# Scan of an RWKV-7 block: the last level of a blockwise inverse writes the turned inverse, without a turn on PE

## What is computed

```python
def wkv7_scan(S0, r, decay, kk, b, k, v, reverse, emit):
    def step(S, inp):
        r_t, w_t, kk_t, b_t, k_t, v_t = inp
        sa = jnp.einsum('bhvk,bhk->bhv', S, -kk_t)
        S = S * w_t[:, :, None, :] + sa[..., None] * b_t[:, :, None, :] + v_t[..., None] * k_t[:, :, None, :]
        y = jnp.einsum('bhvk,bhk->bhv', S, r_t) if emit else None
        return S, y
```

## Time and profile before

| | us |
|---|---|
| median of 3 runs | 4740.95 |
| lowest and highest | 4729.24, 4745.95 |
| profiled execution | 4736.67 |
| its span | 4734.9 |
| the scan in it, first to last PE record | 3108.7 to 3730.6 |

### The profile page before, as it was taken

How to read it: one execution, slowest core, us unless ns; L and a number is a source line. 1 busy time by engine, 2 the same in 40 slices (tenths; PEclk the granted TensorE clock), 3 DMA queues, 4 the chain that set the end, 5 groups by cost and what they waited for, 6 DMA issues and landing times. The chain is left out here.

```text
span 4734.9 us, 81944 instructions
## 1 busy us (share of the span) xinstructions
PE 4130.6 (87%) x34438; PEld 3392.6 (72%) x34438; DVE 2731.4 (58%) x4351; ACT 1748.5 (37%) x2865; POOL 329.5 (7%) x415
## 2 busy tenths in 40 slices
PE   6999986997898998699478897978999587999997
PEld 5878864886785667488366676768888466888886
DVE  2347736884774554789345013657777644466556
ACT  2136623774463442377346111223222112222222
POOL 0000000220000000021000000023233001000000
PEclk9999996998999999799689898969898789999998
DMA  2100037994000002899300201000000031111110
GB/s 100 45 9 2 2 114 292 376 397 147 19 2 1 1 13 98 314 397 382 124 20 19 89 30 59 25 8 3 3 3 3 26 142 54 45 54 36 54 45 40
DMA packets 139161, 425.62 MB, mean 90 GB/s; under 512 B 14660, under 2 KB 50380, under 8 KB 114220
## 3 DMA queue, kind: packets, MB, share of 16 engines
q1 hardware_dynamic: 129580, 386.83, 21.2%
q0 software_dynamic: 9216, 33.56, 2.8%
HBM read 370.03 MB, written 50.33 MB: 89 GB/s over the span
## 5 line engine op out<-in xcount | busy, mean ns | idle before, releaser
L557 PE MATMUL psum<-weight_parts,h_parts 128*128 128x512 f32 (+2 forms) x2880 | 601.0, 371 | 46.0 <-DVE weight_parts L703 29.6
L557 PEld LDWEIGHTS psum<-weight_parts,h_parts 128*128 128x128 f32 x2880 | 508.2, 192 | 132.9 <-DVE weight_parts L703 30.7
L1520 DVE TENSOR_TENSOR weight_parts<-weights_raw,weight_parts 128x2048 fp32r<-128x2048 f32 x192 | 431.8, 2288 | 57.5 <-ACT weight_parts L1490 55.4
L911 ACT ACTIVATE scores<-scores,softmax_stats 128x1024 f32<-128x1024 f32 (+2 forms) x288 | 307.9, 1069 | 329.7 <-DVE softmax_stats L956 329.6
L1490 ACT ACTIVATE weight_parts<-weights_raw 128x2048 fp32r<-128x2048 f32 x192 | 360.6, 1919 | 76.8 <-DMA weights_raw<-in_moe_w_up 46.1
L1428 PE MATMUL psum<-weight_parts,picked_parts 128*128 128x512 f32 x1536 | 365.0, 398 | 16.1 <-DVE weight_parts L1520 10.8
L1901 PE MATMUL psum<-h_parts,up_parts 128*128 128x512 f32 x1536 | 355.5, 393 | 11.0 <-DVE up_parts L1976 11.0
L1917 PE MATMUL psum<-down_parts,hidden_parts 128*128 128x512 f32 x1536 | 353.5, 391 | 6.7 <-DVE down_parts L1981 6.7
L1428 PEld LDWEIGHTS psum<-weight_parts,picked_parts 128*128 128x128 f32 x1536 | 291.5, 191 | 80.1 <-issue 11.5
L703 DVE TENSOR_TENSOR weight_parts<-weights_raw,weight_parts 128x2048 fp32r<-128x2048 f32 (+2 forms) x48 | 100.7, 2098 | 426.5 <-ACT weight_parts L612 426.5
L1901 PEld LDWEIGHTS psum<-h_parts,up_parts 128*128 128x128 f32 x1536 | 291.7, 190 | 72.5 <-DVE up_parts L1976 11.8
(11 more groups left out here) (437 smaller groups left out, 7243.1 us busy)
## 6 DMA issues: line engine op xcount, KB each, us to landing
weights_raw<-in_moe_w_gate SPq DMA_DIRECT2D x64, 1024.0 KB, 14.0
weights_raw<-in_moe_w_up SPq DMA_DIRECT2D x64, 1024.0 KB, 14.1
weights_raw<-in_moe_w_down SPq DMA_DIRECT2D x64, 1024.0 KB, 13.0
w_ada<-in_w_ada SPq DMA_DIRECT2D x12, 2048.0 KB, 11.2
up_raw<-in_w_mlp_up SPq DMA_DIRECT2D x16, 1024.0 KB, 7.2
down_raw<-in_w_mlp_down SPq DMA_DIRECT2D x16, 1024.0 KB, 4.9
weights_raw<-in_even_w_in SPq DMA_DIRECT2D x10, 1024.0 KB, 5.1
weights_raw<-in_w_in SPq DMA_DIRECT2D x10, 1024.0 KB, 5.2
```

Of the source, the lines that this page charges most:

```text
L557: last = pe.matmul(ps[:, t, 0:width(n)], cols[:, i, KP * h + k, t * P:(t + 1) * P], part[:, n % 2, j, k, 0:width(n)], start=(h == 0 and m ...
L911: act.activation(s_b[:, i % 2, a, 0:w], s_b[:, i % 2, a, 0:w], ACT.Exp, bias=st[:, i % 4, 0, a:a + 1], scale=-1.0, accum_out=st[:, i % 4, ...
L1520: dve.tensor_tensor(part[:, n % PART_SLOTS, 1], raw[:, n % RAW_SLOTS], part[:, n % PART_SLOTS, 0].bitcast(F32), ALU.subtract).then_inc(low, 1)
```

## The change

The last level no longer adds its block into `b.M`. What it wants is the inverse turned, and the new block turned is the product of the same two factors with their roles exchanged: the masked X as weights, and columns of `b.MT` as what is multiplied. The masked X of the last level is written into one half of a buffer `XW` of full width (64 columns), whose other half is cleared once by POOL, so that rows of the result that don't belong to the block come out zero. DVE adds the product into the second half of the columns of `b.MT` (`second_half`). The turn on PE, its copy on ACT and the round that both stood in go; `PHASES` goes from 26 to 25, and `LAG` stays 6. The counts of `m_ready` and `mt_ready` trade places (5 and 6 for each tile). POOL and DVE drop one idle round each.

```diff
-PHASES = 26
+PHASES = 25
...
+    WIDE = 115.5
...
+        b.XW = c.at("below_diagonal_wide", WIDE + n, [P, 4, 64])
...
+    first_half = lambda d: slice(32 * d, 32 * d + 32)
+    second_half = lambda d: slice(32 - 32 * d, 64 - 32 * d)
...
                     for level in range(5):
                         n = 5 * i + level
-                        pe.wait_ge(s["m_ready"], n + i + 1)
+                        pe.wait_ge(s["m_ready"], n + 1)
...
+                        if n == 4:
+                            pe.wait_ge(s["x_wide_cleared"], 1)
...
-                        pe.wait_ge(s["mt_ready"], n + 1)
+                        pe.wait_ge(s["mt_ready"], n + i + 1)
                         for h4 in range(4):
                             for cc, C in CH:
-                                last = pe.matmul(ps[C, B, h4 * 32:(h4 + 1) * 32], b.MT[C, h4], b.X[C, h4],
-                                                 start=True, stop=True)
+                                out = ps[C, B, h4 * 32:(h4 + 1) * 32]
+                                if level < 4:
+                                    last = pe.matmul(out, b.MT[C, h4], b.X[C, h4], start=True, stop=True)
+                                else:
+                                    last = pe.matmul(out, b.XW[C, h4], b.MT[C, h4, second_half(d)],
+                                                     start=True, stop=True)
                         last.then_inc(s["m_done"], 1)
                         yield
-                    pe.wait_ge(s["m_ready"], 6 * i + 6)
-                    for h4 in range(4):
-                        for cc, C in CH:
-                            last = pe.matmul(ps[C, A, h4 * 64:(h4 + 1) * 64], b.M[C, h4], c.ident[C, C],
-                                             start=True, stop=True)
-                    last.then_inc(s["mt_turned"], 1)
-                    yield
-                    pe.wait_ge(s["mt_copied"], i + 1)
+                    pe.wait_ge(s["mt_ready"], 6 * i + 6)
...
-                    act.wait_ge(s["mt_turned"], i + 1)
-                    act.activation(flat(b.MT), ps[:, A, 0:256], ACT.Copy).then_inc(s["mt_copied"], 1)
-                    yield
...
+                pool.memset(b.XW[:, :, second_half(d)], 0.0).then_inc(s["x_wide_cleared"], 1)
...
-                    for _ in range(14):
+                    for _ in range(13):
                         yield
...
-                        dve.tensor_tensor(b.X[:], ps[:, A, 0:128].rearrange("p (h n) -> p h n", h=4),
+                        below = b.X[:] if level < 4 else b.XW[:, :, first_half(d)]
+                        dve.tensor_tensor(below, ps[:, A, 0:128].rearrange("p (h n) -> p h n", h=4),
                                           wide(mask.levels[:, level]), ALU.mult).then_inc(s["x_masked"], 1)
...
+                        if level == 4:
+                            dve.wait_ge(s["mt_ready"], 6 * i + 5)
+                            target = b.MT[:, :, second_half(d)]
+                            dve.tensor_tensor(target, target, ps[:, B, 0:128].rearrange("p (h n) -> p h n", h=4),
+                                              ALU.add).then_inc(s["mt_ready"], 1)
```

More of the change, by code:

```diff
@@ L2350, in first_blocks @@
         return v[:, :, d, :] if len(a.shape) == 2 else v[:, :, :, d, :]
+    first_half = lambda d: slice(32 * d, 32 * d + 32)
+    second_half = lambda d: slice(32 - 32 * d, 64 - 32 * d)
     names = ("lora_done", "tanh_done", "log_ready", "running_ready", "exps_ready", "key_scaled", "key_ready", "scaled",
              "ends_scaled", "pairs_done", "pairs_masked", "bk_turned", "bk_copied", "lkv_done", "lkv_copied",
-             "mt_ready", "m_ready", "x_done", "x_masked", "m_done", "mt_turned", "mt_copied", "a_state_done", "z_ready",
+             "mt_ready", "m_ready", "x_done", "x_masked", "x_wide_cleared", "m_done", "a_state_done", "z_ready",
              "u_done", "u_ready", "decayed", "s_done", "state_ready", "y_started", "y_done", "tile_done", "state_cleared")
@@ L2633, in stream @@
                     dve.tensor_tensor(b.MT[:], b.MT[:], wide(eye[:]), ALU.add).then_inc(s["mt_ready"], 1)
-                    dve.wait_ge(s["mt_ready"], 5 * i + 1)
+                    dve.wait_ge(s["mt_ready"], 6 * i + 1)
                     dve.transpose(flat(b.M), flat(b.MT)).then_inc(s["m_ready"], 1)
@@ L2643, in stream @@
                         dve.wait_ge(s["m_done"], n + 1)
[L2644 to L2650, removed]
+                        if level == 4:
[3 more added lines that the diff above has]
+                                              ALU.add).then_inc(s["mt_ready"], 1)
+                        else:
+                            dve.wait_ge(s["m_ready"], n + 1)
+                            target = first_blocks(b.M[:], level, d)
+                            dve.tensor_tensor(target, target, ps[:, B, 0:128]
+                                              .rearrange("p (h g n) -> p h g n", h=4, n=2 << level), ALU.add)\
+                               .then_inc(s["m_ready"], 1)
+                            dve.wait_ge(s["m_ready"], n + 2)
                             dve.transpose(flat(b.MT), flat(b.M)).then_inc(s["mt_ready"], 1)
                         yield
-                    yield
                     for q, cc in enumerate((0, 1) if d == 0 else (1, 0)):
```

## The result

The changed kernel takes 0.987 of the time before (95% interval 0.9859 to 0.9885): medians 4671.5 and 4735.1 us, 61 us by the ratio. The forecast was 4721, its range 4702 to 4752. The profiled execution of the changed kernel took 4685.9 us, with a span of 4684.1; it is the longest of the four shown (the others took 4668.7 to 4673.1), so its rows hold a little more low clock than most executions: the clock over the span is 0.926 in it and 0.930 to 0.932 in the others.

The account below looks back on a forecast made before the run. In the scan neither PE (92% busy) nor DVE (72%) was taken to bound alone; a round lasts about as long as the slower needs. From 4736.7 us, -13.5 for nine tiles, -1 start and -1 tail gave 4721, range 4702 to 4752.

Parts of the forecast that it names:

- DVE's busy time per tile: Sign in the changed kernel's profile, steady part of the scan: DVE's busy time per tile stays at 43 us.
- The level-4 product, its mask and its add: Last level on PE and DVE: same shapes and element counts as before, so no change in time.
- ACT's copy and wait: ACT's 0.38 us copy of the turned inverse and its wait: removal gives nothing in the steady part, something in the tail.
- the weave's term: Scan, 26 rounds becoming 25: -1.3 us a tile, -1.5 with low clock, nine tiles, -13.5.
- table of loads: Sums of PE and DVE work in us for each round of a tile, for 26 and for 25 rounds.
- the one of the two that the text foresaw: Rounds 23 and 24: y's end, 1.75 us of PE, covers the masked pairs; PE's wait for them nearly goes.
- My two sums: Per tile: larger of PE's and DVE's load each round, +0.4 us; over overlapping neighbouring pairs of rounds, halved, -1.3.
- The terms for start and tail: First tile at half clock, double the turn's 0.47 us: -1 us; tail, turn, copy and wait fall away: -1 us.
- rival C: Scan: if rounds 7 to 9 reach 5.3 us, a third low-clock stretch per tile; +15, 4746 to 4765 us, chance 0.18.
- C's measure: Length of stretches with 3.9 us of PE work; for rounds 7 to 9 it decides between 4.6 and 5.3 us.
- each turn would then pay its slot: PE alone sets the pace, each turn gives 0.47 us at full clock: 4702 to 4711 us, chance 0.17.

Follow-up runs that it names:

- filled kernel before: Kernel before, turn and 26 rounds kept, with 16 matmul records that nobody reads added in round 3 of each tile and stream: 0.9943, 27 us faster.
- the last runs: Tiles at full clock: changed kernel with turn's records 52.5 us; same, distances 7, 6, 6, 6, 56.2; filled kernel before 57.0; before with DVE's bt merged, filled, 60.3.

## Why the prediction was wrong, point by point

**What held.** DVE's busy time per tile stayed (43.0 and 42.9 us). The level-4 product, its mask and its add cost what their forerunners did, ACT's copy and wait were free in the steady part (and the run without the copy), and the other stages didn't change.

**The failed step is the weave's term: forecast at -1.3 us a tile (-1.5 with the low clock), measured at -4.5.** At full clock a tile takes 57.0 us with 26 rounds (filled kernel before) and 52.5 with 25; with the low clock of each as it was, 59.6 and 54.0. The term stood in the sum with nine tiles, -13.5; the steady part alone, seven tiles, gave 39.2 us. Two of its inputs can be held against windows.

- By its table of loads rounds 1 to 3 get longer by the 1.1 us that DVE has more to do, and rounds 7 to 9 by 0.7. DVE was busy for 5.22 us in rounds 1 to 3, against 5.43 in the filled kernel before and 5.66 in the kernel before, and for 4.07 us in rounds 7 to 9, against 4.16: the added DVE work didn't fall into these stretches of PE's time.
- By the same table rounds 19 to 21 stay as they are (6.0 us of DVE in both) and the last four rounds lose 1.8 us of PE work as they become three. They fell by 1.0 and by 2.4 us at full clock.

Two waits of PE, in rounds 20 and 24, are gone, and the one between them, in round 22, is down to 0.4 at most. Before, they stood here (timeline of PE, one tile; idle before, and what ended it, in brackets):

```profile
3386.92 0.34 PE L2468 MATMUL psum<-L_k_v,b_and_k_rows 64*64 64x64 f32 x4 [0.37 <-ACT L_k_v L2540]
3390.33 0.50 PE L2459 MATMUL psum<-a_state,inverse_turned 64*64 64x64 f32 x5 [0.59 <-DVE a_state L2657]
...
3398.07 0.41 PE L2406 MATMUL psum<-identity,log_decay 128*128 128x128 f32 x2 [0.57 <-DVE pairs L2624]
```

In the changed kernel the group that needs ACT's U has bk and lora of two other streams ahead of it, and the masked pairs are covered by y's end (1.75 us), which is the one of the two that the text foresaw. How far sums of loads mislead, the last runs tell: weaves with nearly the same loads took 52.5, 56.2, 57.0 and 60.3 us a tile at full clock. My two sums, +0.4 and -1.3, were only 1.7 us apart, far less than such a sum can tell, and the range should have said so. Why the measured weave waits so much less than its loads say stays open beyond these waits.

**The terms for start and tail were too small as well.** They stood at -1 us each, with two tiles at -1.5; the scan is 10.5 us shorter ahead of the steady part and 4.2 behind it, 14.7 against 5. Filler alone, with the turn kept, took 8.5 us off the first of these (117.9 us before, 109.4 filled), at a clock of 0.81 in place of 0.71. The changed kernel is at 0.71 there, as before, so its 10.5 us are not more clock; the sum gave the first tile two slots and no gain from the weave.

**The clock was forecast to stay near 0.91, and only rival C moved it, downwards.** C feared that work taken from PE would bring more low clock. That happens: with the weave unchanged, taking the turn away cut the clock from 0.91 to 0.77 and cost 44 us. But its condition, rounds 7 to 9 as long as 5.3 us, didn't come about (4.5), and in the changed weave the clock of the steady part rose to 0.95. That the shorter waits brought this is argued, not shown. Nor does C's measure, the length of the stretch, hold by itself: in the changed kernel rounds 1 to 3 last 5.6 us in a tile that is at 1.00 from end to end. Of the 61 us, by the ratios: filling the kernel before gives 27, a good part of what low clock cost it; from there to the changed weave with PE's work kept is another 52; and the changed kernel stands 18 behind that one, which is what its remaining low clock costs. 27 + 52 - 18 = 61, where each ratio is known to some 8 us. Some of the 52 is clock as well, since the filled kernel still shows 0.95.

**The rules weighed.** "Perfetto Trace Analysis" (the Trainium skill), section "Identifying the Most-Contended Engine", only says which engine to improve first; that each turn would then pay its slot was the prediction's own step, and it fails: at full clock the changed weave's tile is 52.5 us with the turn's records and 52.5 without. The other page of the Trainium skill that was weighed, "TensorE: Matmul & The Clock Gate", has the clock swing by waits for DMA of 3 to 5 us in the section that the prediction names, and by short idles of PE between groups of matmuls in the next one, "A second HAM failure mode: psum-queue depth-cycling". The traces agree with the second: the waits of the earlier trace rows are 1.0 us at most, and the clock still fell.

## What to carry to other kernels

Where several streams are woven in a fixed order and two engines are both near full, count what an edit does to the order before counting what it removes: a round taken from another place made the kernel 76 us slower instead of 61 faster. Look at the granted clock of the stretch, not of the span; if it is below 1.00, try a few matmuls that nobody reads where PE waits anyway, before any rewrite. Here they brought 27 us to the kernel before, and with the turn's records kept the changed kernel is at its fastest, 0.983 of before.

## What the runs showed of the hardware that was not expected

Removing work can slow a kernel: 640 records less on PE, same order, 44 us more, at a clock of 0.77 instead of 0.91. Adding 640 records for nothing made a kernel 27 us faster (0.91 to 0.95), and 73 us where the clock had been at 0.77. In these four kernels the time that DVE was busy in seven tiles stayed at 301 to 302 us, so it wasn't DVE's work that moved.
